# A streaming encoder layer: the feed-forward part of its first token block computed as seven half-size products per tile pair, its weight sums split straight from SBUF

## The reference

```
def _mlp(x, w_up, w_down):
    return jnp.square(jax.nn.relu(x @ w_up)) @ w_down
...
        hp = hp + _merge(pool_out, attn, gp, ga, w_attn_up[l], w_out[l])
        hp = hp + _mlp(_rmsnorm(hp, norm_mlp[l]), w_up[l], w_down[l])
...
    y_prompt = _rmsnorm(hp, norm_final)
```

## Time and profile before

| what | value |
|---|---|
| median of 3 runs | 2354.0 us (2353.39 to 2355.53) |
| span of the profiled execution, first to last instruction | 2351.3 us |
| PE / DVE / ACT / POOL busy | 99% / 70% / 46% / 15% of the span |
| PE matmuls | 16389 |
| HBM traffic | 410.38 MB by DMA, 175 GB/s in the mean |

### The profile page before, as it was taken

One profiled execution on the slowest core, in us unless ns is written; L12 is line 12 of the kernel. 1 busy time (PEld: TensorE's weight loads), 2 busy tenths in 40 slices (PEclk: granted clock), 3 DMA queues, 4 the chain that ended last, 5 costly groups with the idle time before them and its releaser, 6 DMA issues.

```text
span 2351.3 us, 41109 instructions
## 1 busy us (share of the span) xinstructions
PE 2325.9 (99%) x16389; PEld 2160.8 (92%) x16389; DVE 1642.2 (70%) x2462; ACT 1075.6 (46%) x1898; POOL 350.2 (15%) x272
## 2 busy tenths in 40 slices
PE   8999999999999999999999999999999999999997
PEld 8999999999987889999997788999998778999997
DVE  7645776465985568778687557876788656867766
ACT  4533434233435346456444435654463534645542
POOL 0500364563604000000003200000000400000000
PEclk9999999999999999999999999999999999999998
DMA  4223465565652237766753235767674223676674
GB/s 161 78 74 102 164 233 186 202 240 177 231 183 66 88 117 247 247 210 212 250 186 111 77 103 186 231 208 250 215 258 136 77 88 111 209 242 208 213 253 153
DMA packets 149166, 410.38 MB, mean 175 GB/s; under 512 B 17520, under 2 KB 17872, under 8 KB 144880
## 3 DMA queue, kind: packets, MB, share of 16 engines
q1 hardware_dynamic: 112128, 260.05, 33.9%
q10 hardware_dynamic: 36848, 147.70, 17.8%
HBM read 349.65 MB, written 58.13 MB: 173 GB/s over the span
## 4 chain that ended last, share of the span: by engine, by line
PE 98%; DVE 1%; DMA 1%; ACT 0%; issue 0%; DVEq 0%; SPq 0%; ACTq 0%
PE prod L509 53%; PE auxB L728 8%; PE auxB L729 8%; PE auxB L730 8%; PE prod L728 6%; PE prod L729 6%; PE prod L730 6%; PE auxB L509 1%; PE auxA L611 1%; PE auxB L641 1%; PE auxB L625 1%; PE auxA L509 0%; DMA wring<-weight_split 0%; DVE hT L1241 0%; DMA raw<-weights 0%; DVE wm L1189 0%
## 5 line engine op out<-in xcount | busy, mean ns | idle before, releaser
L509 PE MATMUL prod<-nH,wm 128*128 128x272 f32 (+1 forms) x3104 | 719.7, 333 | 8.2 <-DVE nL L1230 8.2
L509 PEld LDWEIGHTS prod<-nH,wm 128*128 128x128 f32 x3104 | 498.8, 189 | 67.9 <-DVE wm L1189 8.2
L772 ACT ACTIVATE wm<-raw 128x1024 fp32r<-128x1024 f32 x232 | 235.7, 1016 | 693.3 <-PE prod L509 685.2
L509 PE MATMUL prod<-nL,wm 128*128 128x272 f32 (+1 forms) x1552 | 438.8, 331 | 0.0
L772 ACT ACTIVATE wring<-rawq 128x512 fp32r<-128x512 f32 x492 | 303.3, 628 | 256.8 <-PE auxB L730 169.1
L1189 DVE TENSOR_TENSOR wring<-rawq,wring 128x512 fp32r<-128x512 f32 x492 | 334.8, 685 | 97.0 <-PE auxB L730 78.3
L1189 DVE TENSOR_TENSOR wm<-raw,wm 128x1024 fp32r<-128x1024 f32 x232 | 298.9, 1288 | 59.4 <-ACT wm L772 58.5
L509 PE MATMUL prod<-midH,wm 128*128 128x272 f32 (+1 forms) x1664 | 334.7, 313 | 0.2 <-DVE midL L1189 0.2
L509 PEld LDWEIGHTS prod<-nL,wm 128*128 128x128 f32 x1552 | 264.0, 189 | 26.7 <-issue 0.5
L509 PEld LDWEIGHTS prod<-midH,wm 128*128 128x128 f32 x1664 | 253.1, 188 | 18.2 <-issue 0.5
L728 PE MATMUL auxB<-m7H,wring 128*128 128x256 f32 x768 | 217.7, 283 | 0.8 <-DMA wring<-weight_split 0.6
(11 more groups left out here) (172 smaller groups left out, 4352.7 us busy)
## 6 DMA issues: line engine op xcount, KB each, us to landing
raw<-weights SPq DMA_DIRECT2D x200, 512.0 KB, 3.5
wring<-weight_split ACTq DMA_DIRECT2D x171, 512.0 KB, 4.8
rawq<-weights SPq DMA_DIRECT2D x288, 256.0 KB, 3.6
rawq<-weight_sums SPq DMA_DIRECT2D x204, 256.0 KB, 3.9
weight_split<-wsplit ACTq DMA_DIRECT2D x20, 1536.0 KB, 5.6
weight_sums<-wsum ACTq DMA_DIRECT2D x12, 1024.0 KB, 5.3
raw<-weights SPq DMA_DIRECT2D x32, 320.0 KB, 2.8
y<-hT ACTq DMA_DIRECT2D x12, 512.0 KB, 2.8
```

Of the source, the lines that this page charges most:

```text
L509: ins = nc.tensor.matmul(out[:, s, 0:hi - lo], lhs, rhs[:, lo:hi], start=first, stop=last)
L772: return nc.scalar.activation(out, in_, ACT.Copy, scale=scale)
```

## The change

Block 0's MLP is computed with the same seven-product scheme as the others, on halves of 272 columns (`W0`). `plain_up`, `plain_down` and their units are gone. Block 0 has a ring of 7 slots (`RING0`), its own orders for the up phases 2, 4, 6 (`UP0`) and for the down phases (`DOWN0`), and its own step functions on ACT and DVE. All its 224 tokens are split by ACT and DVE. There are no ready sums for it, so:

- The sums of the first four pairs (phase 0) are made during block 0's mixer: SP loads the quarters into four small tiles, POOL forms the sums in place (`sum_early`), SP stores them to `weight_sums`, and block 0 loads them back as tokens.
- From phase 1 on, POOL forms each pair's sums in place from quarters that SP loads into SBUF slots (`load_part`, `sum_weights`, `piece`), and ACT and DVE split tokens from these slots. `wsum` and `wsplit` are gone.
- A split sum that later blocks want is stored by SP directly out of its ring slot once split (`after_split`); ACT's high half for the next user of the slot, seven tokens later, waits for that store (`ring_out`). The stores leave ACT's queue.
- The squares of block 1's input are added by POOL (`add_next_square`), and block 1's input for them is loaded into `x_next` in phase 7.

The diff, cut to its core (ACT and DVE methods that only gain an argument b for the block's width are left out):

```diff
+W0 = CMAX // 2
...
+UP0 = [(0, 1), (0, 5), (0, 2), (0, 6), (0, 3), (0, 7), (1, 1), (1, 5), (0, 4), (1, 6), (1, 3), (1, 2), (1, 7), (2, 1),
+       (2, 5), (1, 4), (2, 6), (2, 3), (2, 2), (2, 7), (3, 1), (3, 5), (3, 2), (3, 6), (3, 3), (3, 7), (2, 4), (3, 4)]
+DOWN0 = [(0, 1), (0, 5), (0, 2), (1, 1), (1, 5), (1, 2), (0, 6), (0, 3), (1, 6), (0, 7), (1, 3), (1, 7), (0, 4), (2, 5),
+         (1, 4), (2, 1), (2, 2), (3, 5), (2, 6), (2, 3), (3, 1), (3, 2), (2, 7), (3, 6), (2, 4), (3, 7), (3, 3), (3, 4)]
...
+        early = [place(f"early{i}", [P, QW], at) for i, at in enumerate(
+            [at_w + half_bytes + 16 * XWMAX + 4 * QW * i for i in range(3)] + [at_z + 12 * CMAX + 8 * XWMAX])]
...
+        for what, ats in (("a21", (at_w + half_bytes - 8 * QW, at_r + 4 * QW, at_acc)),
+                          ("a22", (at_w + half_bytes - 4 * QW, at_r + 8 * QW, at_r + 28 * QW))):
+            for i, at in enumerate(ats):
+                slot_at[what, i] = at
+        slots = {item: place(f"slot_{item[0]}_{item[1]}", [P, QW], at) for item, at in slot_at.items()}
...
+        def ring_slot(b, t):
+            return (4, 5, 6, 7, 0, 1, 2)[t % RING0] if b == 0 else (t + SHIFT[b]) % RING
...
+            def load_part(p, what):
+                ph, j = divmod(p, PAIRS)
+                tile, lo = {"a11": (j, 0), "a12": (j, QW), "a21": (j + PAIRS, 0), "a22": (j + PAIRS, QW)}[what]
+                sp.dma_start(piece(p, what), weights[mlp_row(ph // 2, ph % 2, tile), :, lo:lo + QW]).then_inc(
+                    part_in[slot_of(p, what)], 16)
...
+            def store_sums(p):
+                wait(sp, s_S, p, 3)
+                for r in (3,) if p // PAIRS in SPLIT_PHASES else (7, 6, 5, 3):
+                    sp.dma_start(sums_d[p, :, SUM[r], :], piece(p, part_of[r])).then_inc(sums_out[p % 2], 16)
...
+            def after_split(t):
+                ph = t // NT7
+                j, r = order(0, ph)[t % NT7]
+                p = PAIRS * ph + j
+                wait_split_low(sp, "tok", 0, t)
+                if presplit(ph, r):
+                    slot, at = ring_slot(0, t), SPLIT_PHASES.index(ph) * PAIRS + j
+                    sp.dma_start(split_d[at, :, SUM[r], :, :], f(wring[:, slot, :, :])).then_inc(ring_out[slot], 16)
+                if ph == 0:
+                    return
+                if r == 5:
+                    store_sums(p)
+                if r == 1 and p + 2 <= LAST:
+                    wait(sp, s_S, p, 5)
+                    load_part(p + 2, "a11")
+                if r == 2 and p + 2 <= LAST:
+                    wait(sp, s_S, p, 3)
+                    load_part(p + 2, "a12")
+                if r == 7 and p + 3 <= LAST:
+                    sp.wait_ge(sums_out[p % 2], sums_count[p])
+                    load_part(p + 3, "a21")
+                if r == 4 and p + 3 <= LAST:
+                    load_part(p + 3, "a22")
...
-            def plain_up(q):
...
             def split_high_token(b, t):
-                wait_raw(act, "tok", b, t)
-                copy(wring[:, ring_slot(b, t), 0, :], rawq[:, raw_at["tok", b, t], :]).then_inc(w_high, 1)
+                if b == 0 and t >= RING0 and (t - RING0) in out_count:
+                    act.wait_ge(ring_out[ring_slot(0, t)], out_count[t - RING0])
+                if b > 0 or t < NT7:
+                    wait_raw(act, "tok", b, t)
+                    src = rawq[:, raw_at["tok", b, t], :]
+                else:
+                    ph = t // NT7
+                    j, r = order(0, ph)[t % NT7]
+                    p = PAIRS * ph + j
+                    if r in (1, 2, 4):
+                        act.wait_ge(part_in[slot_of(p, part_of[r])], 16 * use_of(p, part_of[r]))
+                    else:
+                        wait(act, s_S, p, r)
+                    src = piece(p, part_of[r])
+                copy(wring[:, ring_slot(b, t), 0, :], src).then_inc(w_high, 1)
...
+            def up_step0(q, k):
+                if k in (0, 6, 13, 20):
+                    copy_p1(0, q, (k + 1) // 7)
+                if k in (1, 7, 14, 21):
+                    copy_p5(0, q, k // 7)
+                if k in (3, 9, 16, 23):
+                    copy_u2(0, q, k // 7)
+                weights_ahead(0, 2 * q * NT7 + k)
+                if k in (5, 12, 19, 25):
+                    square_z01(0, q, (5, 12, 19, 25).index(k))
+                if k in (6, 13, 20, 26):
+                    square_z2(0, q, (6, 13, 20, 26).index(k))
...
             def split_low_token(b, t):
                 dve.wait_ge(w_high, split_no["tok", b, t])
                 slot = wring[:, ring_slot(b, t)]
-                low(slot[:, 1, :], rawq[:, raw_at["tok", b, t], :], slot[:, 0, :]).then_inc(w_low, 1)
+                if b > 0 or t < NT7:
+                    src = rawq[:, raw_at["tok", b, t], :]
+                else:
+                    j, r = order(0, t // NT7)[t % NT7]
+                    src = piece(PAIRS * (t // NT7) + j, part_of[r])
...
+            def up_step0(q, k):
+                if k == 4:
+                    add_cb(0, q, 0)
+                    relu_z01(0, q, 0)
+                if k == 5:
+                    add_u3(0, q, 0)
+                    relu_z2(0, q, 0)
+                if k == 7:
+                    sum_T13(0, q, 0)
+                    sum_T2(0, q, 0)
+                if k == 8:
+                    relu_z3(0, q, 0)
...
+                if k == 18:
+                    add_cb(0, q, 2)
+                    relu_z01(0, q, 2)
+                if k == 19:
+                    add_u3(0, q, 2)
+                    relu_z2(0, q, 2)
+                    low2(0, q, 1)
...
+                if k == 24:
+                    add_cb(0, q, 3)
+                    relu_z01(0, q, 3)
+                if k == 25:
+                    add_u3(0, q, 3)
+                    relu_z2(0, q, 3)
+                if k == 26:
+                    relu_z3(0, q, 2)
+                    sum_T13(0, q, 3)
+                    sum_T2(0, q, 3)
+                if k == 27:
+                    relu_z3(0, q, 3)
+                    low5(0, q, 3)
+                    sum_T4(0, q, 2)
+                weights_ahead(0, 2 * q * NT7 + k)
+                if k == 27:
+                    low2(0, q, 2)
+                    sum_T4(0, q, 3)
+                    low2(0, q, 3)
...
+            def down_step0(q, k):
+                j, r = DOWN0[k]
+                if r != 2:
+                    add_product(0, q, j, r)
+                weights_ahead(0, (2 * q + 1) * NT7 + k)
+                if q < NQ - 1:
+                    return
+                if k % 2 and 7 <= k < 7 + 2 * KD:
+                    gained_low(1, (k - 7) // 2)
+                if k in (21, 22, 23, 24):
+                    invert_part("x", 1, k - 21)
+                if k == 26:
+                    scale_angles(1)
+                if k in (25, 26):
+                    split_low(1, k - 25)
+                for n, at in ((1, 18), (2, 19), (3, 20), (4, 21), (5, 26), (6, 27), (7, 27)):
+                    if k == at:
+                        add_square("f", 0, n)
 
...
-            def sums_low(n):
...
+            def place_free(p, r):
+                if p >= PAIRS + 2:
+                    ph, j = divmod(p - 2, PAIRS)
+                    wait_split_low(pool, "tok", 0, ph * NT7 + order(0, ph).index((j, r)))
+                elif p == PAIRS + 1:
+                    wait_split_low(pool, "tok", 0, {5: NT7 - 4, 6: NT7 - 3, 3: NT7 - 2}[r])
             def sum_weights(p):
-                a11, a12 = raw[:, first, 0:QW], raw[:, first, QW:2 * QW]
-                a21, a22 = raw[:, second, 0:QW], raw[:, second, QW:2 * QW]
-                link(tt(s[:, 2, :], a11, a21, ALU.subtract))
-                link(tt(s[:, 1, :], s[:, 2, :], a22, ALU.subtract))
-                tt(s[:, 0, :], s[:, 1, :], a11, ALU.subtract)
-                tt(s[:, 3, :], a12, s[:, 1, :], ALU.add).then_inc(s_S.sem, 1)
+                part_landed(p, "a11")
+                part_landed(p, "a21")
+                a21, s6 = piece(p, "a21"), piece(p, "s6")
+                tt(a21, piece(p, "a11"), a21, ALU.subtract).then_inc(s_S.sem, 1)
+                part_landed(p, "a22")
+                if p >= PAIRS + 2:
+                    pool.wait_ge(sums_out[p % 2], sums_count[p - 2])
+                place_free(p, 6)
+                pool.wait_ge(s_S.sem, 4 * (p - PAIRS) + 1)
+                tt(s6, a21, piece(p, "a22"), ALU.subtract).then_inc(s_S.sem, 1)
+                place_free(p, 5)
+                pool.wait_ge(s_S.sem, 4 * (p - PAIRS) + 2)
+                tt(piece(p, "s5"), s6, piece(p, "a11"), ALU.subtract).then_inc(s_S.sem, 1)
+                part_landed(p, "a12")
+                place_free(p, 3)
+                tt(piece(p, "s3"), piece(p, "a12"), s6, ALU.add).then_inc(s_S.sem, 1)
+            def add_next_square(k):
+                wait(pool, s_sq, "x", 1, k)
+                if k > 1:
+                    pool.wait_ge(s_xsum.sem, k - 1)
```

(11 more changed lines are left out.)

652 lines of the change are left out of this document (324 added, 328 removed).

## The result

The changed kernel takes 2396.2 us (median of 4 runs, 2392.5 to 2398.6) where the one before takes 2353.8 on the same chip: ratio 1.0179, 95% interval [1.0165, 1.0194]. It is 1.8% slower; 2341 was forecast, and 2396 lies outside the range. The profiled execution has a span of 2396.5 us, 45.2 more than before.

What follows compares the result with a forecast made beforehand. PE, busy 99% of the span, was taken as the bound: 48.2 us of matmuls saved less 35.5 us of new waits left 12.7 us, a span of 2338.6 and a run of 2341 us, range 2314 to 2364.

Steps and rivals of the forecast that it cites:

- The saving: PE in block 0's MLP: 384 matmuls fewer at 0.1254 us each, 48.2 us saved; 42.1 us a phase.
- The price of a POOL sum: DVE time lost per POOL instruction in block 0's up phases: 0.8 us, between ends 0.38 and 1.1.
- Down phases 1, 3, 5: Block 0's MLP: DVE needs 40 us against PE's 42, PE waits 1.5 us each, 4.5 in all (0 to 9).
- The up phases: Phases 2, 4, 6: DVE's demand 50 us in a 45.4 us window; PE waits 6 us each, 18 in all.
- Phase 7: Last phase of block 0's MLP, with next block's work on DVE: PE waits 5 us (1 to 10).
- case (d): Ring not kept full: stores and quarters late on SP's queue, PE waits for DMA; 2359 us, chance 0.07.
- Phase 0: First phase of block 0's MLP: DVE enters 5.6 us late, PE waits 7 us (2 to 12).
- Phase 1: First down phase of block 0's MLP: 1.5 us of PE waits.
- (a): Block 0's MLP: saving holds, DVE under POOL's turns gives most back; 2341 us, range 2328 to 2352, chance 0.5.
- (b): Block 0's MLP: POOL's sums fall mostly into gaps, 0.38 us each, some 10 us of waits; 2316 us, chance 0.25.
- (c): DVE bounds block 0's MLP: every POOL sum costs 1.1 us, 57 us against 48.2; 2363 us, chance 0.18.
- The last sign: Forecast is wrong at the root if PE's waits sit outside block 0's MLP, or its clock falls in the gaps.

Runs made afterwards that it cites:

- e6: Changed kernel with POOL's 112 sums replaced by memsets of the same 512 columns, sums left out: 2347.7 us, ratio 0.9975 to the kernel before.
- e1: Changed kernel with POOL's 112 sums replaced by 8-column memsets (full width in the first two pairs), waits kept: 2347.8 us, ratio 0.9975 to the kernel before.
- e12: Changed kernel without sums (8-column memsets), all next-block work of phase 7 put behind that phase's last token: 2361.9 us, ratio 1.0035 to the kernel before.
- e3: Changed kernel with phase 7's next-block work (squares, gained tiles, sum of squares, root) moved later, squares and tiles by four steps: 2395.2 us, ratio 1.0180.
- e7: Changed kernel without sums (8-column memsets), x_next loaded in four pieces two steps apart, squares three steps later, gained tiles two: 2344.0 us, ratio 0.9958.
- e9: e7 plus 28 extra matmuls of 272 columns at each of three PE waits (phases 0, 1, 7): 2344.9 us, ratio 0.9965 to the kernel before.

## Why the prediction was wrong

**The saving** was right: 384 matmuls, 0.1254 us each, and the inner phases without sums run at 43.5 to 43.7 us against my 42.1, 1.4 a phase that I had not counted.

**The price of a POOL sum** was right: 0.78 against 0.8, inside 0.38 to 1.1. Their number was a little low: 14 to 16 POOL instructions stand in an up phase where I had 12 to 13, about 2 us more of DVE's time. The Trainium skill, "SBUF — State Buffer", section "Who interferes with whom", says that two-input Vector work contends with GpSimd work that reads SBUF and not with work that only writes it; e6 agrees, since its memsets left splits at 0.684 us.

**The place where that price falls** was wrong, and this is the first step that failed: "Down phases 1, 3, 5 ... 40 against 42 ... I take 1.5 us each". Measured are 11.2, 7.3 and 5.1 above 42.1, 23.6 in place of 4.5. I let half of the 15 POOL instructions hit. DVE is busy 45.5 us in phase 3 and 33.0 in e1's, 12.5 for 18 POOL instructions, 0.7 each, so nearly all hit. An up phase's backlog of 3 to 6 us is carried in even without sums (e1's up phases are busy 37.2 us where I counted 40.1, its down phases 33.0 where I counted 26.5). The up phases lost 9.7, 11.7 and 10.9 us, 32 in place of 18. I had subtracted DVE's demand from its window, as if an instruction that is late could be made up anywhere in the phase. But PE waits for single instructions: eight times for the addition of P5, up to 3.6 us. In e1 nearly all of it is gone: the sums cost 37.4 us in the inner phases, which lost 44.6 in all where 21 were forecast (18 in the ups and 3 in two of the downs).

**Phase 7** was the second failed step: "39.2 ... I take 5 (1 to 10)"; it lost 22.7. My count of DVE's work was fair (39.2 and up to 6 inherited; it is busy 46.5 in e1), but the longest waits of phase 7 come through ACT's order. Its waits in phase 7 of the changed kernel (ACT's timeline; wait in brackets):

```profile
652.31 0.63 ACT L910 ACTIVATE sq<-x_next 128x512 f32<-128x512 f32 x1 [8.72 <-DMA x_next<-x]
662.54 0.63 ACT L910 ACTIVATE sq<-x_next 128x512 f32<-128x512 f32 x1 [7.44 <-POOL work L1822]
```

```profile
668.91 0.56 PE L831 MATMUL auxB<-m0H,wring 128*128 128x272 f32 x1 [5.71 <-DVE hT L1703]
```

ACT stood first for x_next, then for a square sum that POOL does only after the last pair's sums, which waited for a quarter behind x_next (POOL stood 9.3 us for it). Behind ACT's square stood the high half of a weight, behind that DVE's split, behind that DVE's addition, and PE. I never listed what stands behind the wait for x_next, and wrote of ACT only that it had time. e12 gives the next block's work 11.6 of the 18 us that phase 7 loses without sums; e3 and e7 show that moving it by a few steps saves none or little of it (1 us, within the spread, and 3.8). Of the other 6.4 us, 3.0 are a wait behind which late stores out of the ring stand: case (d), which I had priced at zero. No run took the load of x_next away.

**Phase 0** lost 14.5 in place of 7, inside my bounds (2 to 12) only without the sums (e1: 9.2). What I called case (d), a ring store that comes late, happened there: in e1, ACT's timeline:

```profile
276.05 0.63 ACT L872 ACTIVATE wring<-rawq 128x512 fp32r<-128x512 f32 x1 [3.38 <-DMA weight_split<-wring]
...
280.53 0.71 ACT L916 ACTIVATE rms<-auxA,eps 128x544 f32<-128x544 f32 x1
```

That store took 6.8 us to land, the next one 7.4, in a phase with DMA at 0.86, where I had reckoned 4.8 to 5.6. The root behind it in ACT's order came at 280.5, DVE's 3.6 us reciprocal after it, and PE waited 4.4 us for a split. That the late store caused the whole of PE's wait is read from the order of the rows; no run took the store away. **Phase 1** begins with a wait for a split (4.7 us in e1, 4.0 in the changed kernel) that stands behind phase 0's last four low halves on DVE. I had given it 1.5.

**The clock** was not in my sum, only in its last sentence. In the windows of the changed kernel PE is idle for 61 us and busy for 369; e1's undisturbed inner phases are busy 42.6 each, so at most 28 of the 369 are the price of the lower clock (1.2 in place of 2.4 GHz). Phases 2, 3 and 5 are busy 1.1 to 1.5 us more at a clock of 1.00, so it is less: what the eight granted clocks lack of 1.00, times each phase's length, is 21 us. By this estimate the 93 us are some 54 of added waits, 21 to 28 of clock, and 11 that even a quiet phase takes above 42.1 (43.5), with what is left of the 28. e9 shows that the price is real (2.3 us behind one wait), and that extra work gives it back at one place of three only.

**The cases.** (a) and (b) fell with the terms above. (c), "DVE is the bound of block 0's MLP", named the mechanism, but tied it to a price of 1.0 us and more; the waits it stands for came at 0.78. The last sign, that I am wrong at the root if the clock falls in the gaps, came true. Even with no sums at all the kernel is 5.0 us faster than before (e1) and 9.5 with x_next spread (e7): the whole prize was small, since phases 0, 1 and 7 alone give back 35 us of the 48. No version that computes everything beat the kernel before.

## What to carry to other kernels

An engine that is 95% loaded makes its neighbour wait long before 100%: work out for each product which single instruction it waits for and what stands ahead of that one, not the phase's sum of work. Where sums on GpSimd run beside a nearly full VectorE, count each of them against it (0.78 us each here). Moving them to VectorE returned little here (7.6 of 48 us): they then stand in line with its own work. And an in-order engine's wait for a large load belongs in the forecast with everything behind it, also on an engine that is half idle; so do the stores that stand behind that load in its queue.

## What was not expected of the hardware

- A two-input GpSimd sum slowed even 128-column VectorE subtractions from 0.284 to 0.62 us; a GpSimd memset of 512 columns beside 512-column subtractions cost them nothing (0.684 us).
- In e7, waits of PE of 4.0 to 4.7 us were followed by windows of 6 us at a mean granted clock of 0.60 to 0.73; the one worked out cost 2.3 us beyond its own length. 28 extra matmuls ahead of a wait kept the clock at 1.00 at two places, and a phase grew shorter at one of them.
- Stores of 512 KB out of the ring took 6.8 and 7.4 us to land in e1 at the start of phase 0, and 9.4 and 9.9 us in e12 behind the load of x_next; the median before was 5.6 for stores three times as large.
